# Inverse roots of the differential tiles by VectorE instead of a reciprocal and a ScalarE square root

## The chip, the core and the metric

The kernel runs on one core of a Trainium2 chip. The core has five engines with queues of their own: TensorE (PE, matmuls), VectorE (DVE), ScalarE (ACT, activation functions), GpSimd (POOL) and SyncE (SP, issues DMAs). They meet only at semaphores. The metric is the device time of one execution in microseconds; lower is better.

## The reference, cut to what matters

Two transformer blocks follow each other on a sequence of 512 tokens of width 1024, all in float32. The second block has three attention branches; one is differential attention with 4 heads of value width 64:

```python
def diff_branch(dq, dk, dv, pos, qn_g, kn_g, lam_vecs, subln_g, lam_init):
    ...
    def block_fn(qblk, start):
        sc = jnp.einsum('bqhmd,bkhmd->bhmqk', qblk, k).astype(jnp.float32) * scale
        sc = jnp.where(causal_mask(start, s)[None, None, None], sc, NEG_INF)
        p = jax.nn.softmax(sc, axis=-1)
        a = (p[:, :, 0] - lam * p[:, :, 1]).astype(v.dtype)
        return jnp.einsum('bhqk,bkhd->bqhd', a, v)

    o = causal_block_sweep(block_fn, q)
    o = rms_norm(o, subln_g) * (1.0 - lam_init)
    return o.reshape(b, s, DIFF_W)
```

`rms_norm` divides each head's 64 values of a token by the root of their mean square plus 1e-6. It is the inverse root of this last norm that the change computes in another way. The branch's output then goes with those of latent attention (8 heads) and memory attention (4 heads) through a gate and the output projection.

## The kernel before, in words

The program is one instruction stream per engine, written out by hand; the order in each stream is the order in the code, and semaphores (`wait_ge`, `then_inc`) order the engines against each other. `link` puts a wait for VectorE's own step counter behind an instruction, so that the next one may read its result. Weights come as 128x1024 units through RAW, split by ScalarE (WHI) and GpSimd (WLO) into a high and a low half, so that a float32 product is made of three TensorE passes (lines 1838 to 1840).

The change lies in the last stage but one, `attention("late")`. Its list LATE has 20 maps: 8 of latent heads, 8 of differential heads (two for each head) and 4 of memory heads. A loop counter i runs over the maps, and each engine does in step i the work of several maps at different stages:

- TensorE: scores of map i+2 (lines 1977, 1982, or 1838 to 1840), the transposes of map i's probabilities (line 2010), value matmuls of map i-1 (lines 2038, 2043).
- VectorE: bias and row maximum of map i+1 (`biased`, line 1347), which also reads the scores out of their PSUM bank, so that TensorE may write the next ones; then `normed` of map i (lines 1362, 1387, 1389); then what concerns finished maps (1265, 1462, 1464).
- ScalarE: copies of the transposed probabilities of map i-1 (line 875), exponentials of map i+1 (line 902), copies of finished outputs (945, 951).
- GpSimd: the widest scaling of a map (lines 685, 719, 725).

Two differential heads share a 128x512 tile, with the features in rows. There are two such tiles, and `diff_tile` names the step at which each is worked on. For a tile, ScalarE squares it (948); TensorE sums the squares over each head's 64 rows, turned so that tokens lie in partitions and SS gets 8 columns (2097, `dm_tot`); VectorE makes mean plus epsilon (1469) and the reciprocal (1470, `dm_rin`); ScalarE takes the root and spreads it by a broadcast of each column to 64 (862, into YSQ, `dm_rstd`); TensorE turns that back with an identity (2081, `dm_spread`); VectorE multiplies the tile by it and the gain (1413), then by the gate and a constant (1416, `dm_y`); ScalarE copies the high half (937, `dm_hi`), and VectorE makes the low one (1454, which the profile shows under the helper's line 1265). On ScalarE, line 862 stands at the head of its step, ahead of 875 and 902. On VectorE, lines 1469 and 1470 stand at the end of theirs, just ahead of the next map's bias adds. On TensorE, line 2081 stands behind the scores of map i+2.

ScalarE computes a function from a table that has to be loaded; the compiler puts an ACT_TABLE_LOAD ahead of an activation whose function isn't in the table loaded last.

Of the kernel before, what the change touches and what calls it, by code (L numbers as in the profile page):

```python
# [17 lines left out]
I32 = mybir.dt.int32  # L18
ALU = mybir.AluOpType
ACT = mybir.ActivationFunctionType  # L20
AX = mybir.AxisListType

P = 128
# [74 lines left out]
class Chain:  # L98
# [5 lines left out]
    def link(self, ins):  # L104
        self.n += 1
        ins.then_inc(self.sem, 1)
        self.eng.wait_ge(self.sem, self.n)


def build(nc, t, out):  # L110
    from contextlib import ExitStack
    ctx = ExitStack()
    with ctx:
# [41 lines left out]
        SS = sb("SS", [P, 64])  # L155
# [18 lines left out]
        YT, YSQ = PB[:, 5 * SEQ:6 * SEQ], PB[:, 6 * SEQ:7 * SEQ]  # L174
# [26 lines left out]
        def row(name, n):  # L201
# [46 lines left out]
        dm_sq, dm_tot, dm_rin, dm_rstd, dm_spread, dm_read, dm_y, dm_hi, dm_lo, k_mm = [sem(s) for s in  # L248
            ("dm_sq", "dm_tot", "dm_rin", "dm_rstd", "dm_spread", "dm_read", "dm_y", "dm_hi", "dm_lo", "k_mm")]
# [78 lines left out]
        for h in range(4):  # L328
            for m in range(2):
# [4 lines left out]
                               y=h, rows=slice(64 * (h % 2), 64 * (h % 2) + 64), ytile=Y_DM + h // 2, ztile=4 + h // 2,  # L334
# [9 lines left out]
        for h in range(NH):  # L344
# [4 lines left out]
                            y=h, rows=slice(64 * (h % 2), 64 * (h % 2) + 64), ytile=LQ + h // 2, ztile=h // 2,  # L349
# [5 lines left out]
        for maps in (ab, LATE):  # L355
            n = ng = nt = 0
# [374 lines left out]
        def _(act):  # L731
# [44 lines left out]
            for kt in range(KT):  # L776
                if kt == 2:
# [3 lines left out]
                    for b in range(5):  # L781
                        a, e = OH * b // 5, OH * (b + 1) // 5
                        ins = act.activation(FX[0:16, :, :].rearrange("p a b -> p (a b)")[:, a:e], PS[0:16, 2 + b, 0:e - a], ACT.Copy)
# [16 lines left out]
            for c in range(13):  # L800
                if c != 1:
                    stream(u + (c + 3 if c else 4))
                if c < 11:
# [5 lines left out]
                    else:  # L809
                        for g in range(2 if c == 8 else 1):  # L810
                            for half in (slice(0, 64), slice(64, 128)):
                                ins = act.activation(hi(K_AT[c][g])[half, :], ps[64 * g:64 * g + 64, :], ACT.Copy)
                        if c > 8:
                            ins = act.activation(key_raw(c), ps[64:128, :], ACT.Copy)
# [24 lines left out]
            for tk in range(NT):  # L839
                ins = act.activation(GATE[:, tk, :], PS[:, 4 + tk, 384:408], ACT.Sigmoid, scale=RT[:, tk:tk + 1])  # L840
# [14 lines left out]
            def attention(name):  # L855
                maps, pts = GROUP[name]
                A = ATT[name]
                for i in range(-1, len(maps) + (3 if name == "late" else 2)):
                    tile = diff_tile(maps, i - 4)
                    if tile is not None:  # L860
                        act.wait_ge(dm_rin, tile + 1)
                        act.activation(YSQ.rearrange("p (g e) -> p g e", g=8), SS[:, 0:8, None].broadcast_to([P, 8, 64]),
                                       ACT.Sqrt).then_inc(dm_rstd, 1)
                    if 0 <= i - 1 < len(maps) and maps[i - 1].get("mode") != "hold":
                        m = maps[i - 1]
                        if m["n"] > 2:
# [4 lines left out]
                        for g, qs in enumerate(m["groups"]):  # L871
                            act.wait_ge(A["turned"], m["t0"] + g + 1)
                            for q in [q for q in qs if q <= 4]:
                                for to, src in turned_aps(m, pt, q):
                                    ins = act.activation(to, src, ACT.Copy)  # L875
# [4 lines left out]
                    if name == "ab" and i == 2:  # L880
                        act.wait_ge(cmp_mm, 1)
                        for g in range(2):
                            kc = slice(KC + 32 * g, KC + 32 * g + 32)
                            for half in (slice(0, 64), slice(64, 128)):
                                ins = act.activation(hi(22)[half, kc], PS[64 * g:64 * g + 64, 2, 32 * g:32 * g + 32], ACT.Copy)
                        ins.then_inc(cmp_hi, 1)
                    if name == "ab" and i == LATE_K:
                        act.wait_ge(A["scores"], ab[8]["g0"])
                        for ktile in (9, 10):
                            for half in (slice(0, 64), slice(64, 128)):  # L890
                                ins = act.activation(hi(K_AT[ktile][1])[half, :], key_raw(ktile), ACT.Copy)
                            ins.then_inc(late_hi, 1)
                    if i + 1 < len(maps):
                        m = maps[i + 1]
                        for g, qs in enumerate(m["groups"]):
                            act.wait_ge(A["biased"], m["g0"] + g + 1)
                            if 4 in qs:
                                ins = act.activation(prob_cmp(m), prob_cmp(m), ACT.Exp, scale=m["scale"])
                            for q in [q for q in qs if q < 4]:
                                nk = m["spans"][q][1]  # L900
                                dst = prob_of(m, q)
                                ins = act.activation(dst, dst, ACT.Exp, bias=stat(m, NMAX)[:, q:q + 1], scale=-1.0,  # L902
                                                     accum_out=stat(m, SUM)[:, q:q + 1])
                        if m.get("sink"):
                            ins = act.activation(stat(m, SINK), stat(m, NMAX), ACT.Exp,
                                                 bias=row("sinks", 8)[:, m["h"]:m["h"] + 1])
# [14 lines left out]
                    if name == "ab" and 0 <= i - 2 < len(maps) and maps[i - 2]["last"]:  # L921
# [3 lines left out]
                        for half, qs in halves(m):  # L925
                            ins = act.activation(blocks_of(yt[rows, :], qs), blocks_of(PS[half:half + DH, m["bank"], :], qs), ACT.Copy)
# [274 lines left out]
        def _(dve):  # L1201
            chain = Chain(dve, dve_step)
            link = chain.link
# [37 lines left out]
            for kt in range(KT):  # L1241
                dve.wait_ge(n_hi, kt + 1)
                dve.scalar_tensor_tensor(out=HLO[:, kt, :], in0=X[:, kt, :], scalar=col("g_mix", kt),  # L1243
                                         in1=HHI[:, kt, :].bitcast(F), op0=ALU.mult, op1=ALU.subtract).then_inc(n_lo, 1)
# [22 lines left out]
            for c in range(11):  # L1267
# [9 lines left out]
                else:  # L1277
                    for g in range(2 if c == 8 else 1):
                        rows = slice(64 * g, 64 * g + 64)
                        for half in (slice(0, 64), slice(64, 128)):  # L1280
                            ins = low_from_psum(lo(K_AT[c][g])[half, :], hi(K_AT[c][g])[rows, :], ps[rows, :])
# [69 lines left out]
            def normed(A, m):  # L1351
# [24 lines left out]
                for qs in m["groups"][:2] if "latent" in m else m["groups"][:1] if "pair" in m else m["groups"]:  # L1376
# [12 lines left out]
                            ins = dve.tensor_scalar(ap, ap, w, None, ALU.mult)  # L1389
                    ins.then_inc(A["normed"], 1)  # L1390

            def attention(name):
                maps, pts = GROUP[name]
                A = ATT[name]
                for i in range(-1, len(maps) + 3):
# [5 lines left out]
                    if name == "ab" and i == 2:  # L1401
# [5 lines left out]
                        for q in range(NT):  # L1407
                            ins = dve.tensor_copy(v_cmp(q)[32 * q:32 * q + 32, :], PS[0:32, 2, P:2 * P])
                        ins.then_inc(cmp_lo, 1)
                    tile = diff_tile(maps, i - 4)  # L1410
                    if tile is not None:
                        dve.wait_ge(dm_spread, tile + 1)
                        dve.scalar_tensor_tensor(out=YT, in0=YT, scalar=col("subln"), in1=PS[:, DIFF_BANK[tile], :],
                                                 op0=ALU.mult, op1=ALU.mult).then_inc(dm_read, 1)
                        dve.wait_ge(dm_read, tile + 1)
                        dve.scalar_tensor_tensor(out=YT, in0=YT, scalar=1.0 - LAM_INIT, in1=FX[:, 4 + tile, :],
                                                 op0=ALU.mult, op1=ALU.mult).then_inc(dm_y, 1)
# [5 lines left out]
                    if name == "ab" and 0 <= i - 3 < len(maps) and maps[i - 3]["last"]:  # L1423
# [3 lines left out]
                        for half, qs in halves(m):  # L1427
                            ins = low_from_psum(blocks_of(yl[rows, :], qs), blocks_of(yh[rows, :], qs),
                                                blocks_of(PS[half:half + DH, m["bank"], :], qs))
# [13 lines left out]
                    if name == "ab" and i - 1 in UA_FILL:  # L1443
                        n = UA_FILL[i - 1]
# [21 lines left out]
                    if diff_tile(maps, i - 3) is not None:  # L1466
                        tile = diff_tile(maps, i - 3)
                        dve.wait_ge(dm_tot, tile + 1)
                        link(dve.tensor_scalar(SS[:, 0:8], PS[:, DIFF_BANK[tile], 0:8], 1.0 / 64, EPS, ALU.mult, ALU.add))
                        dve.reciprocal(SS[:, 0:8], SS[:, 0:8]).then_inc(dm_rin, 1)  # L1470

            attention("ab")


# [21 lines left out]
            for j in range(4):  # L1496
# [20 lines left out]
                for e in range(2):  # L1517
                    dve.wait_ge(merge_act, 4 * j + 3 + e)
                    n = 14 + 2 * j + e
# [909 lines left out]
```

## Time and profile before

| | |
|---|---|
| median of 3 runs | 1075.66 us (1074.31 to 1080.67) |
| profiled execution, its own time | 1074.28 us |
| its span | 1072.4 us |
| TensorE busy | 1025.3 us, 96% |
| VectorE busy | 606.8 us, 57% |
| ScalarE busy | 544.7 us, 51% |
| GpSimd busy | 407.8 us, 38% |
| mean granted TensorE clock | 0.987 |

The span is the time from the first to the last instruction in the profile of one execution; the execution's own time has 1.9 us around it. Busy shares are averages over stages with different limits. Line numbers are those of the kernel before.

### The profile page before, as it was taken

The numbers are of one execution on the slowest core, as the hardware profiler recorded it, in microseconds if no ns is written. First come the engines' busy times: TensorE is split into PE (matmuls) and PEld (weight loads), VectorE is DVE, ScalarE is ACT, GpSimd is POOL, SyncE is SP. The second block draws the span as 40 slices with busy tenths as digits, with TensorE's granted clock in tenths as the row PEclk, the third lists the DMA queues.
The fourth block names the chain that finished last, engine by engine and source line by source line (L and its number), as shares of the span: only waits on it lengthen the run. The fifth ranks groups of instructions, "written<-read, shape, count | busy, mean of one in ns | idle before, by whom it ended". The sixth has DMA issues, their size and how long they took to land.

```text
span 1072.4 us, 15098 instructions
## 1 busy us (share of the span) xinstructions
PE 1025.3 (96%) x5166; PEld 837.8 (78%) x5166; DVE 606.8 (57%) x1327; ACT 544.7 (51%) x1104; POOL 407.8 (38%) x211
## 2 busy tenths in 40 slices
PE   6999999999999999999999999999999889888798
PEld 4879788888778788888888888788887778666577
DVE  4547457988364665554545454433334988586732
ACT  5443666887433345444444444443334463977921
POOL 2456412001243444444444444415443334533332
PEclk9999999999999999999999999999999999899999
DMA  7564222111134322222222224233443134332213
GB/s 259 194 169 153 84 79 74 51 41 40 41 119 132 110 93 96 99 98 98 98 98 98 91 101 141 99 138 98 153 132 99 59 109 127 94 89 74 73 56 118
DMA packets 38812, 111.88 MB, mean 104 GB/s; under 512 B 5235, under 2 KB 8563, under 8 KB 38067
## 3 DMA queue, kind: packets, MB, share of 16 engines
q1 hardware_dynamic: 28572, 87.60, 25.1%
q10 hardware_dynamic: 8584, 18.89, 5.5%
q0 software_dynamic: 1600, 4.66, 1.2%
q8 instruction: 33, 0.54, 0.2%
q14 instruction: 23, 0.19, 0.1%
HBM read 100.25 MB, written 7.96 MB: 101 GB/s over the span
## 4 chain that ended last, share of the span: by engine, by line
issue 49%; PE 21%; POOL 14%; DVE 8%; ACT 5%; DMA 3%; POOLq 0%; ACTq 0%; DVEq 0%
POOL WLO L668 13%; PE PS L1838 6%; PE PS L1840 6%; PE PS L1839 6%; DMA RAW<-wstream 2%; ACT PB L902 1%; PE PS L2038 1%; ACT WHI L741 1%; PE PS L2188 1%; DMA X<-xT 1%; ACT HF L875 1%; PE PS L2010 1%; DVE PB L1387 1%; DVE PB L1347 1%; DVE FX L1647 1%
## 5 line engine op out<-in xcount | busy, mean ns | idle before, releaser
L668 POOL TENSOR_TENSOR WLO<-RAW,WHI 128x1024 fp32r<-128x1024 f32 x147 | 355.2, 2417 | 585.2 <-ACT WHI L741 585.0
L741 ACT ACTIVATE WHI<-RAW 128x1024 fp32r<-128x1024 f32 x154 | 162.8, 1058 | 282.1 <-PE PS L1840 261.6
L1838 PE MATMUL PS<-HHI,WHI 128*128 128x512 f32 x648 | 256.9, 396 | 9.9 <-DVE HLO L1243 8.6
L1840 PE MATMUL PS<-HHI,WLO 128*128 128x512 f32 x648 | 254.2, 392 | 0.0
L1839 PE MATMUL PS<-HLO,WHI 128*128 128x512 f32 x648 | 254.0, 392 | 0.0
L1838 PEld LDWEIGHTS PS<-HHI,WHI 128*128 128x128 f32 x648 | 123.0, 190 | 38.9 <-issue 12.1
L1838 PE MATMUL PS<-BHI,WHI 128*128 128x512 f32 x368 | 145.3, 395 | 3.5 <-POOL WLO L668 2.0
L1840 PE MATMUL PS<-BHI,WLO 128*128 128x512 f32 x368 | 143.4, 390 | 0.0
L1839 PE MATMUL PS<-BLO,WHI 128*128 128x512 f32 x368 | 143.3, 389 | 0.0
L1840 PEld LDWEIGHTS PS<-HHI,WLO 128*128 128x128 f32 x648 | 122.6, 189 | 26.1
L1839 PEld LDWEIGHTS PS<-HLO,WHI 128*128 128x128 f32 x648 | 123.0, 190 | 25.2 <-issue 0.5
L1225 DVE TENSOR_TENSOR PS<-PS,PB 128x512 f32<-128x512 f32 x63 | 43.9, 696 | 85.4 <-PE PS L1840 83.8
L1838 PEld LDWEIGHTS PS<-BHI,WHI 128*128 128x128 f32 x368 | 69.1, 188 | 21.1 <-issue 2.5
L1840 PEld LDWEIGHTS PS<-BHI,WLO 128*128 128x128 f32 x368 | 69.1, 188 | 14.7
L1839 PEld LDWEIGHTS PS<-BLO,WHI 128*128 128x128 f32 x368 | 69.2, 188 | 13.8
L902 ACT ACTIVATE PB<-PB,ST 128x256 f32<-128x256 f32 (+3 forms) x132 | 69.6, 544 | 0.6 <-DVE ST L1347 0.5
L1561 DVE SCALAR_TENSOR_TENSOR FX<-PS,CL,FX 128x511 f32<-128x511 f32 (+1 forms) x88 | 61.6, 742 | 13.4 <-ACT FX L1001 13.2
L2010 PE MATMUL PS<-IDN,PB 128*128 128x128 f32 x270 | 40.4, 291 | 11.3 <-DVE PB L1389 6.5
L1838 PE MATMUL PS<-WHI,HHI 128*128 128x512 f32 (+2 forms) x128 | 48.0, 375 | 2.7 <-ACT PB L1027 2.0
L1840 PE MATMUL PS<-WHI,HLO 128*128 128x512 f32 (+2 forms) x128 | 47.4, 370 | 0.0
L1839 PE MATMUL PS<-WLO,HHI 128*128 128x512 f32 (+2 forms) x128 | 47.3, 369 | 0.0
L2010 PEld LDWEIGHTS PS<-IDN,PB 128*128 128x128 f32 x270 | 32.7, 148 | 18.5 <-DVE PB L1389 5.3
(332 smaller groups left out, 1504.1 us busy)
## 6 DMA issues: line engine op xcount, KB each, us to landing
RAW<-wstream SPq DMA_DIRECT2D x154, 512.0 KB, 3.2
X<-xT ACTq DMA_DIRECT2D x4, 512.0 KB, 9.2
BF<-wstream POOLq DMA_DIRECT2D x2, 1024.0 KB, 6.7
BG<-wstream POOLq DMA_DIRECT2D x2, 1024.0 KB, 7.1
bias_b<-bias_rows ACTq DMA_DIRECT2D x2, 1024.0 KB
FX<-bias_b ACTq DMA_DIRECT2D x8, 256.0 KB, 2.6
X<-xT ACTq DMA_DIRECT2D x8, 256.0 KB, 3.6
x_keep<-X ACTq DMA_DIRECT2D x2, 1024.0 KB, 6.5
```

Of the source, the lines that this page charges most:

```text
L668: pool.tensor_tensor(WLO[:, s, :], RAW[:, s, :], WHI[:, s, :].bitcast(F), ALU.subtract).then_inc(split_lo, 1)
L741: act.activation(WHI[:, c % 2, :], RAW[:, c % 2, :], ACT.Copy).then_inc(split_hi, 1)
L875: ins = act.activation(to, src, ACT.Copy)
L902: ins = act.activation(dst, dst, ACT.Exp, bias=stat(m, NMAX)[:, q:q + 1], scale=-1.0, accum_out=stat(m, SUM)[:, q:q + 1])
L1225: dve.tensor_tensor(PS[:, bank, :], PS[:, bank, :], RSTD, ALU.mult).then_inc(scaled, 1)
L1347: ins = dve.tensor_tensor_reduce(prob_of(m, q), PS[:, b, o:o + nk], bias_of(m, q), -m["scale"], init, ALU.add, ALU.min, stat(m, NMAX)[:, q ...
L1387: ins = dve.scalar_tensor_tensor(out=ap, in0=ap, scalar=w, in1=o, op0=ALU.mult, op1=ALU.add)
L1561: dve.scalar_tensor_tensor(out=y, in0=PS[:, 2 * e + s, 0:SEQ - sh], scalar=cv[:, tap:tap + 1], in1=y, op0=ALU.mult, op1=ALU.add).then_inc( ...
L1838: pe.matmul(dst, a[0], b[0], start=first, stop=False, **kw)
L1839: pe.matmul(dst, a[0], b[1], start=False, stop=False, **kw)
L1840: return pe.matmul(dst, a[1], b[0], start=False, stop=last, **kw)
L2010: ins = pe.transpose(PS[:, 3 + b, o + j * P:o + (j + 1) * P], pr[:, p0:p0 + P], IDN[:, :])
```

## The change

The root moves to VectorE. A new helper `inverse_root` takes a first value of the inverse root from the number's bits read as an integer (-0.5 times the bits plus a constant), and improves it in three Newton steps of three operations each. VectorE thus issues ten operations on 128x8 where it issued one reciprocal, and each but the last is linked. The result is in columns 8 to 15 of SS, and columns 16 to 23 are scratch. ScalarE's line 862 becomes a Copy with the same broadcast, of 128x512.

```diff
@@ -859,8 +859,8 @@
                         act.wait_ge(dm_rin, tile + 1)
-                        act.activation(YSQ.rearrange("p (g e) -> p g e", g=8), SS[:, 0:8, None].broadcast_to([P, 8, 64]),
-                                       ACT.Sqrt).then_inc(dm_rstd, 1)
+                        act.activation(YSQ.rearrange("p (g e) -> p g e", g=8), SS[:, 8:16, None].broadcast_to([P, 8, 64]),
+                                       ACT.Copy).then_inc(dm_rstd, 1)
@@ -1389,6 +1389,17 @@
+            def inverse_root(x, y, t):
+
+                link(dve.tensor_scalar(y.bitcast(I32), x.bitcast(I32), -0.5, float(0x5F3759DF), ALU.mult, ALU.add))
+                for n in range(3):
+                    link(dve.tensor_tensor(t, y, y, ALU.mult))
+                    link(dve.scalar_tensor_tensor(out=t, in0=t, scalar=-0.5, in1=x, op0=ALU.mult, op1=ALU.mult))
+                    ins = dve.scalar_tensor_tensor(out=y, in0=t, scalar=1.5, in1=y, op0=ALU.add, op1=ALU.mult)
+                    if n < 2:
+                        link(ins)
+                return ins
+
@@ -1467,7 +1478,8 @@
                         link(dve.tensor_scalar(SS[:, 0:8], PS[:, DIFF_BANK[tile], 0:8], 1.0 / 64, EPS, ALU.mult, ALU.add))
-                        dve.reciprocal(SS[:, 0:8], SS[:, 0:8]).then_inc(dm_rin, 1)
+                        root = inverse_root(SS[:, 0:8], SS[:, 8:16], SS[:, 16:24])
+                        root.then_inc(dm_rin, 1)
```

ScalarE's instructions around the first differential tile, before (YSQ is a part of PB; HF takes the turned probabilities):

```order
L951 ACTIVATE BHI<-PS 64x512
L862 ACT_TABLE_LOAD
L862 ACTIVATE PB<-SS 128x512
L875 ACTIVATE HF<-PS 128x2x128
L875 ACTIVATE HF<-PS 128x128
L875 ACTIVATE HF<-PS 128x3x128 x2
L875 ACTIVATE HF<-PS 128x128
L902 ACT_TABLE_LOAD
L902 ACTIVATE PB,ST<-PB,ST 128x256
```

and of the change at the same place:

```order
L951 ACTIVATE BHI<-PS 64x512
L862 ACTIVATE PB<-SS 128x512
L875 ACTIVATE HF<-PS 128x2x128
L875 ACTIVATE HF<-PS 128x128
L875 ACTIVATE HF<-PS 128x3x128 x2
L875 ACTIVATE HF<-PS 128x128
L902 ACTIVATE PB,ST<-PB,ST 128x256
```

Both table loads are gone; the second tile loses its two in the same way, and all else is in the same order.

VectorE at the first tile, before (L1347 is the bias add and maximum of the next map):

```order
L1464 TENSOR_TENSOR PS<-PS,FX 64x256
L1469 TENSOR_SCALAR SS<-PS 128x8
L1470 RECIPROCAL SS<-SS 128x8
L1347 ISA PB,ST<-PS,TRI 128x256
L1347 ISA ST 128x1
```

and of the change, where lines behind the new helper have numbers higher by 11:

```order
L1480 TENSOR_SCALAR SS<-PS 128x8
L1394 TENSOR_SCALAR SS<-SS 128x8
L1396 TENSOR_TENSOR SS<-SS 128x8
L1397 SCALAR_TENSOR_TENSOR SS<-SS 128x8
L1398 SCALAR_TENSOR_TENSOR SS<-SS 128x8
L1396 TENSOR_TENSOR SS<-SS 128x8
L1397 SCALAR_TENSOR_TENSOR SS<-SS 128x8
L1398 SCALAR_TENSOR_TENSOR SS<-SS 128x8
L1396 TENSOR_TENSOR SS<-SS 128x8
L1397 SCALAR_TENSOR_TENSOR SS<-SS 128x8
L1398 SCALAR_TENSOR_TENSOR SS<-SS 128x8
L1347 ISA PB,ST<-PS,TRI 128x256
```

The ten operations stand where the reciprocal stood, ahead of the bias adds in VectorE's queue.

## Rows read from the trace of the kernel before

**Rows 1.** ScalarE's instruction groups: line, operation, count, busy us, mean ns, idle before.

```profile
L862 ACT ACT_TABLE_LOAD x2 | 2.6, 1283 | 0.0
```

**Rows 2.** The chain of waits, 974 to 1013 us: start, length, what it went through.

```profile
975.15 0.39 ACT L862
975.54 0.90 issue
...
978.46 1.28 ACT L902
...
983.20 0.42 DVE PB L1347
...
985.11 4.28 POOL PB L719 x4
...
1004.76 1.11 ACT L862
...
1007.79 1.28 ACT L902
...
1012.44 0.43 DVE PS L1462
```

**Rows 3.** Timeline of tile 1: start, length, instruction, idle before and its releaser.

```profile
975.08 0.17 DVE L1469 TENSOR_SCALAR SS<-PS 128x8 f32<-128x8 f32 x1 [0.63 <-PE PS L2097]
...
975.28 0.20 DVE L1470 RECIPROCAL SS<-SS 128x8 f32<-128x8 f32 x1
975.43 0.42 DVE L1347 CUSTOM_DVE_ANT_0 PB<-PS,TRI 128x256 f32<-128x256 f32 x1
...
977.08 0.08 DVE L1347 DVE_READ_ACCUMULATOR2_ANT ST<- 128x1 f32 x1
...
977.22 0.29 PEld L1982 LDWEIGHTS PS<-BLO,BHI 128*128 128x128 f32 x1 [0.32 <-DVE ST L1347]
...
977.38 2.04 PEld L2081 LDWEIGHTS PS<-IDN,PB 128*128 128x128 f32 x8
...
979.76 0.75 DVE L1413 SCALAR_TENSOR_TENSOR PB<-PB,CL,PS 128x512 f32<-128x512 f32 x1 [1.59 <-PE PS L2081]
...
980.54 0.69 DVE L1416 SCALAR_TENSOR_TENSOR PB<-PB,FX 128x512 f32<-128x512 f32 x1
...
981.95 0.61 ACT L937 ACTIVATE BHI<-PB 128x512 fp32r<-128x512 f32 x1
...
982.59 0.69 DVE L1265 TENSOR_TENSOR BLO<-PB,BHI 128x512 fp32r<-128x512 f32 x1 [0.77 <-ACT BHI L937]
```

**Rows 4.** Timeline of tile 2.

```profile
1005.61 0.20 DVE L1470 RECIPROCAL SS<-SS 128x8 f32<-128x8 f32 x1
...
1007.11 0.08 DVE L1347 DVE_READ_ACCUMULATOR2_ANT ST<- 128x1 f32 x1
...
1007.46 0.19 PEld L1838 LDWEIGHTS PS<-BHI 96*128 96x128 f32 x1
...
1008.10 1.09 PEld L2081 LDWEIGHTS PS<-IDN,PB 128*128 128x128 f32 x8
...
1009.42 0.75 DVE L1413 SCALAR_TENSOR_TENSOR PB<-PB,CL,PS 128x512 f32<-128x512 f32 x1 [1.49 <-PE PS L2081]
...
1010.81 0.68 DVE L1265 TENSOR_TENSOR BLO<-PS,BHI 64x512 fp32r<-64x512 f32 x1
...
1011.63 1.08 PE L2038 MATMUL PS<-HF,BF 128*64 128x256 f32 x8 [1.07 <-DVE BLO L1265]
```

**Rows 5.** Timeline of VectorE in the rope angles, a linked chain of small operations.

```profile
296.98 0.23 DVE L1488 SCALAR_TENSOR_TENSOR COS<-KR,COS 128x64 f32<-128x64 f32 x1
297.24 0.49 DVE L1490 SCALAR_TENSOR_TENSOR COS<-KR,COS 128x64 f32<-128x64 f32 x2
```

**Rows 6.** Busy us in two stretches, then granted clock (PEclk), DMA share, GB/s.

```profile
978.00:980.00 2.00, 2.00 (x12) 2.00 (x11) 0.41 (x2) 1.97 (x4) 1.51 (x1) 0.50 0.16 66
...
1008.00:1010.00 2.00, 1.92 (x16) 1.59 (x15) 0.58 (x1) 1.99 (x5) 1.82 (x2) 1.00 0.00 0
```

## The prediction

> **What bounds the kernel now.** I read the page first. Over the whole span TensorE is the busiest engine, but the edited lines run in one short stage, the late attention (about 924 to 1025 us), so that stage decides, not the span's shares. Next came the instruction groups of ScalarE. Line 862, the edited one, carries two table loads of 1.28 us [rows 1]; with a square root gone from between exponentials, its return load goes too. Then the chain of waits through the two places where line 862 runs. There the chain is mostly ScalarE's: at the first place the load of line 862 and the wait for it take 0.39 + 0.90 us, and the exponentials behind it pay 1.28 us for getting their table back; at the second 1.11 and 1.28 us [rows 2]. So four loads lie on the chain as it stands, and a reader may be tempted to book them as gain. The timeline of the two places shows what runs just beside that chain [rows 3, 4]. I call the places tile 1 (975 to 983 us) and tile 2 (1005 to 1012 us).
>
> In tile 1 VectorE makes mean plus epsilon at 975.08 and the reciprocal at 975.28, and from 975.43 the bias adds of the next map (line 1347). Their last accumulator read ends at 977.16. TensorE's last score matmul waits for just that (0.32 us idle, released by ST of line 1347), and its next work, at 977.38, is line 2081, which spreads the roots. VectorE's line 1413 waits 1.59 us for line 2081, then comes 1416, then ScalarE's 937, then VectorE's copy of the low half, then the next bias adds at 983.20, which stand on the chain [rows 2, 3]. A second path, VectorE to TensorE to VectorE, thus runs beside ScalarE's with little slack. This is the path that the edit lengthens.
>
> **The change, part by part.** *Table loads removed.* Copy runs between exponentials without a load already (line 875 does, all through the stage), and the instruction order has no load left there: four fewer, 4 x 1.28 = 5.1 us of ScalarE busy time. The load of line 862 was partly hidden, though: it began at 975.15, and the reciprocal that ScalarE waited for anyway ended only at 975.48 [rows 2, 3].
>
> After each load the next activation starts within 0.02 us: 978.46 + 1.28 gives 979.74, and the exponentials start at 979.75 in the chain. The Trainium skill (ScalarE: Activation LUTs, "What ACT_TABLE_LOAD costs") says 1283 ns for the load and some 1380 ns of drain besides, 2.66 us for a switch. The load agrees with the row; by the drain, ScalarE's path would win 1.38 us more in each tile than I book. The trace shows no such gap here, so by that rule my sum would be wrong on ScalarE's path alone.
>
> *Ten VectorE instructions for one.* The reciprocal (0.20 us) is replaced by ten operations on 128x8, nine of them followed by a wait for VectorE's own semaphore. A step of this kind takes 0.20 us from start to start: 975.08 to 975.28, duration 0.17 [rows 3]. The bounds are 0.17 (its duration, no gap) and 0.26 (a linked scalar-tensor-tensor of 128x64, 296.98 to 297.24 [rows 5]); I take 0.20, since width and engine fit. The tenth operation has nothing chained to it, like the reciprocal now, and takes its place (0.15 to the next start). So VectorE reaches the bias adds 9 x 0.20 = 1.80 us later, and ScalarE's release comes at 975.28 + 1.80 + 0.17 = 977.25 and 1007.58 instead of 975.48 and 1005.81.
>
> *ScalarE's path.* Line 862 starts 0.08 us after the release: 977.33 against 976.44 now, +0.89; the return load is gone, -1.30; the exponentials start 0.41 us earlier. In tile 2: 1007.66 against 1006.05, +1.61 - 1.30 = 0.31 us later [rows 2, 4]. On this path alone the change is worth -0.1 us: it swaps its waits.
>
> *VectorE's queue.* Behind the chain stand the bias adds, which free score banks for TensorE. In TensorE's order the scores come ahead of line 2081, so the spread waits for them though its input is ready. **Tile 1:** bias end 977.16 to 978.96, line 2081 to 979.18, line 1413 from 979.76 to 981.56, line 1416's end from 981.23 to 983.03. ScalarE's 937 now starts at 981.95, held by ScalarE's own work, 0.72 us after its input; it will start at 983.11, +1.16. The low half and the bias adds at 983.20 move with it [rows 3]. From there the chain goes through VectorE to GpSimd's four scalings (4.28 us) and on, without room that I can see, so **+1.16** is carried to tile 2 [rows 2]. **Tile 2:** bias end 1007.19 to 1008.99; the score matmuls that need it start now at 1007.46 (0.27 us after, TensorE was busy until then), and would at 1009.04: +1.58. With it go line 2081 (1008.10), 1413 (1009.42), the low half at 1010.81, the value matmuls at 1011.63 that waited 1.07 us for it, and line 1462 at 1012.44, on the chain [rows 2, 4]: **+1.58**. Behind it VectorE is the bound up to the output projection, which is dense TensorE work and carries the shift to the end.
>
> Sum: 1.16 + 1.58 = **+2.7 us**. Nothing else moves: TensorE, GpSimd and the DMA queues issue what they did, and the scratch columns 8 to 23 of SS are used by nobody then.
>
> Against the profiled execution (1074.28 us) that is 1077.0. The median of the three runs is 1.4 us above that execution, which would give 1078.4. I say 1077.5, between the two.
>
> **Rivals.**
> *A, ScalarE's path decides* (-0.1 to +1.7). Where the shifted TensorE work finishes sooner than I move it, ScalarE sets the time. There is something for it: in tile 1 the granted clock around line 2081 was 0.50, in tile 2 it was 1.00 [rows 6], and its load-weights span was 2.04 us against 1.09 [rows 3, 4]. 0.50 is the 1.2 GHz level, 1.00 is 2.4; TensorE had waited for bias adds just before. If 1.80 us later the clock is back, 0.95 us of tile 1's shift is returned: 0.2 + 1.6 = +1.8, 1076.1. If tile 2 also finds cover, 1074.2. Against: in tile 2 the line was at full clock already and has no second to return.
> *B, slower still: the clock falls in tile 2.* The edit makes TensorE wait 1.6 us more before line 2081 there. If the clock then drops as it did in tile 1, line 2081 takes 0.95 us longer on the path: +3.7, and with steps of 0.26 instead of 0.20 (0.54 more in each tile) +4.7: 1078.0 to 1079.0, or 1080.4 from the median. It decides where the granted clock between 1006 and 1012 falls to 0.50; it is the case on the slower side, should my forecast count as no change.
> *C, faster: the loads on the chain are simply gone.* 0.39 + 1.28 + 1.11 + 1.28 = 4.06 us [rows 2] gives 1070.2. It needs the VectorE chain to be free and the path over 2081 to have 2 us of slack, from the point where line 862 starts before 976. The timeline speaks against both: VectorE ran nothing beside the chain that could be postponed, and line 937's slack is 0.72 us.
> *D, the loads stay*, the compiler putting one at the copy. The instruction order shows none; then ScalarE's own path is 0.89 and 1.61 us late beside the other (1.16 and 1.58), +2.8 us, 1077.1.
>
> **How the numbers follow.** My forecast 45%, A 28%, B 18%, C 5%, D 1%, the rest for what I do not see. About 1% (10.8 us) is what a measurement of this kernel can tell from no change: its three runs lie 6.4 us apart. All cases lie inside that, so no change takes nearly everything: 0.97, with 0.015 for each side. The range goes from A's best, 1074.2 less a few tenths for the runs' scatter, to B from the median: 1073.8 to 1080.4. It leaves out C and a run as high as the highest of the three.
>
> **What the profile after would show.** Right: two fewer table loads at line 862 and two fewer at 902; ten operations of 0.17 to 0.2 us, their starts 0.20 apart; line 862 at some 977.3, waiting idle on VectorE for about 2 us; the exponentials at 979.3; line 937 now idle on VectorE, and the bias adds of 983.20 at 984.3; line 1462 of tile 2 at 1015.2 (1012.44 + 2.7). Wrong: line 1413 starting within 1 us of today's time (then A), a clock of 0.50 in tile 2 (B), or steps over 0.26 us. The forecast as a whole fails if the span moves by more than 5 us in either direction, since no term here reaches that far.

## The result, and the profile after

| | before | the change |
|---|---|---|
| median of 8 runs | 1076.01 us (1074.31 to 1080.67) | 1080.24 us (1078.49 to 1082.71) |
| profiled execution, its own time | 1074.28 us | 1080.1 us |
| its span | 1072.4 us | 1078.3 us |
| VectorE busy | 606.8 us | 610.0 us |
| ScalarE busy | 544.7 us | 539.4 us |
| mean granted TensorE clock | 0.987 | 0.976 |

The ratio is 1.0046, with a 95% interval of 1.0034 to 1.0058. That is 4.9 us more (1076 x 0.0046), between 3.7 and 6.2. The change is slower, by less than 1%. The forecast had 1077.5, 1.8 us above the median it started from. It had the direction, and less than half of the size.

The edit itself came out as written. In ScalarE's groups of the kernel after, line 862 has no table load any more, and line 902 has two where the kernel before had four:

```profile
L902 ACT ACT_TABLE_LOAD x2 | 2.6, 1283 | 0.0
```

The timeline of tile 1 after (lines behind the helper are 11 or 12 higher; 1480 is the old 1469, 1994 the old 1982, 2093 the old 2081, 1424 the old 1413), to be read against [rows 3]:

```profile
974.55 0.17 DVE L1480 TENSOR_SCALAR SS<-PS 128x8 f32<-128x8 f32 x1 [0.63 <-PE PS L2109]
974.75 0.17 DVE L1394 TENSOR_SCALAR SS<-SS 128x8 int32<-128x8 int32 x1
...
974.96 0.17 DVE L1396 TENSOR_TENSOR SS<-SS 128x8 f32<-128x8 f32 x1
975.16 0.17 DVE L1397 SCALAR_TENSOR_TENSOR SS<-SS 128x8 f32<-128x8 f32 x1
...
976.56 0.17 DVE L1398 SCALAR_TENSOR_TENSOR SS<-SS 128x8 f32<-128x8 f32 x1
976.71 0.42 DVE L1347 CUSTOM_DVE_ANT_0 PB<-PS,TRI 128x256 f32<-128x256 f32 x1
976.76 0.63 ACT L862 ACTIVATE PB<-SS 128x512 f32<-128x512 f32 x1 [2.16 <-DVE SS L1398]
...
977.20 0.29 PEld L1994 LDWEIGHTS PS<-BLO,BHI 128*128 128x128 f32 x1 [2.77 <-DVE ST L1347]
...
978.66 2.04 PEld L2093 LDWEIGHTS PS<-IDN,PB 128*128 128x128 f32 x8
...
981.03 0.75 DVE L1424 SCALAR_TENSOR_TENSOR PB<-PB,CL,PS 128x512 f32<-128x512 f32 x1 [1.59 <-PE PS L2093]
...
982.54 0.63 ACT L937 ACTIVATE BHI<-PB 128x512 fp32r<-128x512 f32 x1 [1.62 <-DVE PB L1427]
...
983.81 0.42 DVE L1347 CUSTOM_DVE_ANT_0 PB<-PS,TRI 128x256 f32<-128x256 f32 x1
```

The ten operations take 0.17 us each and start 0.20 us apart, as forecast. ScalarE waits 2.16 us idle ahead of line 862. TensorE's weight loads, which waited 0.96 us before the first scores, now wait 2.77 us. The row of before for that:

```profile
975.91 0.19 PEld L1982 LDWEIGHTS PS<-BLO,BHI 128*128 128x128 f32 x1 [0.96 <-DVE ST L1347]
```

From the mean plus epsilon to the bias adds of the next step it was 983.20 - 975.08 = 8.12 us; it is 983.81 - 974.55 = 9.26 us. That is +1.14 where the prediction had +1.16.

The chain of waits after, in tile 1, no longer goes through ScalarE's table loads and exponentials [rows 2]. It goes through VectorE's queue and TensorE:

```profile
977.88 1.41 PE PS L1994 x3
979.29 1.72 PE PS L2093 x8
...
981.03 0.76 DVE PB L1424
...
981.82 0.70 DVE PB L1427
...
982.54 0.64 ACT BHI L937
```

Tile 2 after, by the timeline, against [rows 4]:

```profile
1007.48 0.17 DVE L1480 TENSOR_SCALAR SS<-PS 128x8 f32<-128x8 f32 x1 [1.94 <-PE PS L2109]
...
1010.44 0.29 PEld L1850 LDWEIGHTS PS<-BHI 96*128 96x128 f32 x1 [1.64 <-DVE ST L1347]
...
1011.90 0.33 PEld L1850 LDWEIGHTS PS<-BHI 96*128 96x128 f32 x1
...
1013.07 2.04 PEld L2093 LDWEIGHTS PS<-IDN,PB 128*128 128x128 f32 x8
...
1015.44 0.75 DVE L1424 SCALAR_TENSOR_TENSOR PB<-PB,CL,PS 128x512 f32<-128x512 f32 x1 [3.62 <-PE PS L2093]
```

Here much more was lost. From mean plus epsilon to line 1413's multiplication of the tile (now 1424) it was 1009.42 - 1005.41 = 4.01 us; it is 1015.44 - 1007.48 = 7.96 us, +3.95 where I forecast +1.58. A weight load of the scores takes 0.33 us instead of 0.19, and line 2093's loads take 2.04 us instead of 1.09. Busy times and granted clock in stretches of 2 us (busy us of TensorE, weight loads, VectorE, ScalarE, GpSimd; then the granted clock) show at what clock this work ran, and show a further low stretch that I had not expected, at 993:

```profile
992.00:994.00 2.00, 0.83 (x6) 0.53 (x5) 1.92 (x8) 0.92 (x3) 0.00 (x0) 0.75 0.00 0
994.00:996.00 2.00, 2.00 (x10) 2.00 (x11) 1.93 (x9) 2.00 (x10) 0.96 (x1) 0.50 0.41 70
...
1008.00:1010.00 2.00, 1.02 (x9) 0.42 (x4) 1.73 (x12) 0.31 (x1) 0.00 (x0) 1.00 0.00 0
1010.00:1012.00 2.00, 1.55 (x6) 1.56 (x7) 1.78 (x11) 2.00 (x8) 0.09 (x1) 0.51 0.00 0
1012.00:1014.00 2.00, 2.00 (x8) 1.71 (x7) 0.00 (x0) 1.36 (x6) 1.74 (x2) 0.50 0.00 0
1014.00:1016.00 2.00, 2.00 (x11) 2.00 (x11) 0.56 (x1) 0.00 (x0) 0.00 (x0) 0.50 0.00 0
```

Around line 2081 of tile 2 the clock was 1.00 before [rows 6]. After, TensorE is busy for 1.02 of the 2 us from 1008, and when it starts again at 1010.4 the clock is 0.50, 1.2 instead of 2.4 GHz, until about 1016.8. The work that runs at half the clock is the path: scores, then 2093, on which VectorE waits 3.62 us with everything behind it.

Three lengths per profile divide what follows tile 1, and I use them for all runs: from mean plus epsilon of tile 1 to that of tile 2, from there to the first matmul of the output projection, and from there to the end (47.0 to 47.1 us in every run). Each is the difference of two starts in that run's timeline. Each profile is one execution, so a single difference of a few tenths of a us says little.

| profile | tile 1 to tile 2 | tile 2 to projection |
|---|---|---|
| before | 30.33 | 19.93 |
| the change | 32.93 | 23.75 |

### The profile page after: what moved, and what is told of

It is laid out like the page before. It is cut to its first block, busy times and chain, and to the rows that moved or that the text cites. A ratio compares the mean times of both kernels' runs of the same rounds, so it can differ in the third digit from the quotient of the medians.

```text
span 1078.3 us, 15112 instructions
## 1 busy us (share of the span) xinstructions
PE 1030.6 (96%) x5166; PEld 843.6 (78%) x5166; DVE 610.0 (57%) x1345; ACT 539.4 (50%) x1100; POOL 408.0 (38%) x211
## 3 DMA queue, kind: packets, MB, share of 16 engines
HBM read 100.25 MB, written 7.96 MB: 100 GB/s over the span
## 4 chain that ended last, share of the span: by engine, by line
issue 48%; PE 25%; POOL 14%; DVE 8%; ACT 2%; DMA 2%; POOLq 0%; ACTq 0%; DVEq 0%
POOL WLO L668 13%; PE PS L1850 7%; PE PS L1852 6%; PE PS L1851 6%; PE PS L2022 1%; PE PS L2050 1%; PE PS L2200 1%; DMA RAW<-wstream 1%; DVE PB L1347 1%; DMA X<-xT 1%; PE PS L2055 1%; ACT WHI L741 1%; DVE PB L1387 1%; DVE FX L1659 1%; DVE FX L1655 0%
```

## The experiments

The theory after the result, called theory A in the texts below (it is not rival A of the prediction): the loads lie beside the path and are worth next to nothing; the ten operations delay VectorE's queue and through it TensorE (2.7 us); and TensorE's longer wait makes the granted clock fall in work on the path (the rest). The rivals: the loads do count, and something else costs yet more (their rival B); or the change has a fixed price whatever the length of the chain; or the clock has no part. All ratios are to runs of the kernel before on the same chip, and 0.001 is 1.08 us.

### Each half alone

`loads_only` leaves out the root: the reciprocal of before stays on VectorE, and only this changes:

```diff
-                                       ACT.Sqrt).then_inc(dm_rstd, 1)
+                                       ACT.Copy).then_inc(dm_rstd, 1)
```

> The reciprocal of before, spread by a Copy instead of a Sqrt: the roots are left out, so the four table loads are gone and nothing is added to VectorE. Theory A (VectorE's queue sets the path, the loads lie beside it): ScalarE comes 0.9 us earlier at tile 1's exponentials and line 937 can start at most 0.7 us earlier there and 0.1 us in tile 2, so -0.8 us against before (ratio 0.999). Rival B (the loads on the chain are worth what the chain says): -4 us (ratio 0.996).

Measured: 0.9995 (0.9981 to 1.0008), -0.5 us. Four table loads, 5.1 us of ScalarE, are worth 2 us at most (the interval's lower end), against the 4 us of the chain. In its tile 1 line 937, which ScalarE's own work held by 0.72 us before, waits 0.78 us for VectorE:

```profile
978.28 0.20 DVE L1470 RECIPROCAL SS<-SS 128x8 f32<-128x8 f32 x1
...
978.52 0.63 ACT L862 ACTIVATE PB<-SS 128x512 f32<-128x512 f32 x1 [0.39 <-DVE SS L1470]
...
980.32 1.29 PEld L2081 LDWEIGHTS PS<-IDN,PB 128*128 128x128 f32 x8
...
983.46 0.63 ACT L937 ACTIVATE BHI<-PB 128x512 fp32r<-128x512 f32 x1 [0.78 <-DVE PB L1416]
```

In this profile the next bias adds come 984.73 - 978.08 = 6.65 us after mean plus epsilon, where before it was 8.12. About half of that gain is not the table loads': the clock was still 1.00 when line 2081 began, its weight loads took 1.29 us instead of 2.04, and line 1413 started 3.87 us after mean plus epsilon instead of 4.68. The other half is the slack ahead of line 937, so removing the table loads does gain something here, but little; over the whole kernel it does not stand out from the noise.

`chain_only`: the change, but line 862 stays a Sqrt, of columns 8 to 15, so that what it spreads is not the inverse root:

```diff
-                                       ACT.Copy).then_inc(dm_rstd, 1)
+                                       ACT.Sqrt).then_inc(dm_rstd, 1)
```

> The ten VectorE operations of the change, but line 862 stays a Sqrt (so what it spreads isn't the inverse root), and the four table loads stay. Theory A: the loads are hidden beside VectorE's path, so this is as slow as the change, before +4.2 us (ratio 1.004), within 0.7 us of it. Rival B: the change as it is got 1 to 4 us back from the loads, so without that this is before +5 to +8 us (ratio 1.005 to 1.0075).

Measured: 1.0038 (1.0020 to 1.0056), +4.1 us. With its table loads back the kernel is as slow as the change (1.0046) and not slower, so no gain from the loads' removal shows beside the chain (the two intervals leave room for 1 to 2 us). In tile 2 the load runs at 1010.13 to 1011.41 and line 862 starts at 1013.13, idle before it, because VectorE's tenth operation ends only at 1013.10:

```profile
1010.13 1.28 ACT L862 ACT_TABLE_LOAD   x1
...
1012.93 0.17 DVE L1398 SCALAR_TENSOR_TENSOR SS<-SS 128x8 f32<-128x8 f32 x1
1013.13 0.63 ACT L862 ACTIVATE PB<-SS 128x512 f32<-128x512 f32 x1 [1.72 <-DVE SS L1398]
```

### Each tile alone

The change in one of the two tiles, the other as before (`tile == 0` for tile 1, `tile == 1` for tile 2; line 862 is a Copy of columns 8 to 15 in the changed tile and a Sqrt of columns 0 to 7 in the other, which the cut below leaves out):

```diff
-                        root = inverse_root(SS[:, 0:8], SS[:, 8:16], SS[:, 16:24])
+                        root = inverse_root(SS[:, 0:8], SS[:, 8:16], SS[:, 16:24]) if tile == 0 else dve.reciprocal(SS[:, 0:8], SS[:, 0:8])
```

> The change made in tile 1 alone; tile 2 keeps reciprocal and Sqrt. Theory A with a lowered clock: 1.2 us of shift through VectorE's queue, and some 1 to 1.5 us more where the longer idle time of TensorE makes the granted clock fall in the stage behind it: +1.2 to +2.5 us. Without the clock's part: +1.2 us. Rival B: 0 or below, since two loads go.

> The change made in tile 2 alone. Theory A with a lowered clock: 1.6 us of shift, and 1.5 to 2.4 us more because the clock falls while line 2081 of tile 2 runs (2.0 us instead of 1.1 for its weight loads): +2.5 to +4 us, and a granted clock of 0.50 there. Without the clock's part: +1.6 us and a clock of 1.00 there.

Measured: tile 1 alone 1.0018 (1.0003 to 1.0032), +1.9 us; tile 2 alone 1.0030 (1.0011 to 1.0048), +3.2 us. Together 5.1, and the change is 4.9. The profiles:

| profile | tile 1 to tile 2 | tile 2 to projection |
|---|---|---|
| before | 30.33 | 19.93 |
| tile1_only | 31.47 (+1.14) | 20.07 |
| tile2_only | 30.63 | 22.13 (+2.20) |

In the profiles, tile 1 costs what the queue alone should cost, and tile 2 costs 0.6 us more than its 1.58. The profile of tile2_only has the low clock in tile 2:

```profile
1010.00:1012.00 2.00, 2.00 (x13) 1.87 (x13) 1.14 (x7) 2.00 (x8) 0.73 (x1) 0.92 0.00 0
1012.00:1014.00 2.00, 2.00 (x12) 2.00 (x11) 0.79 (x2) 0.71 (x4) 1.09 (x2) 0.50 0.00 0
1014.00:1016.00 2.00, 1.46 (x10) 1.00 (x11) 1.90 (x3) 0.63 (x1) 0.00 (x0) 0.72 0.00 0
```

Here TensorE takes up the scores again at 1009.80, and the clock falls only at about 1011.7; in the change it had fallen before the scores went on. So only line 2081 (here 2094) is slow:

```profile
1009.80 0.19 PEld L1851 LDWEIGHTS PS<-BHI 96*128 96x128 f32 x1 [1.64 <-DVE ST L1348]
...
1011.22 1.62 PEld L2094 LDWEIGHTS PS<-IDN,PB 128*128 128x128 f32 x8
```

Line 2094 starts 4.38 us after mean plus epsilon, against 2.69 us for line 2081 before: +1.69, which is the queue's part, measured while the clock was 1.00. In chain_only it is 4.40, with the fall at about 1015.5 and loads of 1.90 us. In the change it is 5.59, because there the scores were slow too. The size of tile 2's loss thus depends on where the fall lands.

### The length of the chain

One Newton step, and six (the cut shows the first; the second has 6 and 5 in these places):

```diff
-                for n in range(3):
+                for n in range(1):
...
-                    if n < 2:
+                    if n < 0:
```

> The change with one Newton step instead of three (four operations for the reciprocal; the root is less exact). VectorE's bias adds come 3 x 0.20 = 0.6 us late. Theory A: line 937's slack of 0.7 us in tile 1 covers it, tile 2 gets 0.4 us: before +0.4 us, -0.5 to +1 with the load's gain on ScalarE. Rival (a fixed cost of the change, whatever its length): before +3 to +4 us.

> The change with six Newton steps (19 operations): bias adds 18 x 0.20 = 3.6 us late. Theory A: 1.8 us more in each tile than the change, +3.6 us, so before +7.8 us, up to +9.5 if the clock stays low for longer. Rival (another wait than VectorE's queue sets the path, such as ScalarE's loads): less than 2 us more than the change.

Measured: one step 1.0004 (0.9992 to 1.0016), +0.4 us; six steps 1.0073 (1.0056 to 1.0090), +7.9 us. Both as theory A had them. From 4 to 10 to 19 operations the time goes +0.4, +4.9, +7.9. A fixed price of the change is out. The price is not even per operation either. In tile 1 the first 0.6 us of delay are free, by the slack ahead of line 937: the next bias adds of one_step come 8.07 us after mean plus epsilon, 8.12 before. From 4 to 10 operations the queue grows by 2.4 us over both tiles, and the time by 4.5; from 10 to 19 it grows by 3.6 us, and the time by 3.0. The profiles show what was added between 4 and 10: in tile 2 the clock is 1.00 up to line 1413 with one step, and falls ahead of it with three and with six.

### Keeping TensorE busy in the wait

Two matmuls that nothing reads, in the change and (as a control) in the kernel before, ahead of the scores of the step in question. They wait until VectorE has read the bank (`SUMS_READ` holds its step count there; the trace has two records for each such matmul):

```diff
+            def keep_busy(tile, n):
+                pe.wait_ge(dve_step, SUMS_READ[tile])
+                for _ in range(n):
+                    pe.matmul(PS[:, DIFF_BANK[tile], 128:512], IDN[:, :], TRI[:, 128:512], start=True, stop=True,
+                              skip_group_check=True)
...
+                    if diff_tile(maps, i - 4) is not None:
+                        keep_busy(diff_tile(maps, i - 4), 2)
                     if 0 <= i + 2 < len(maps):
                         scores(A, maps[i + 2])
```

> The change, with two matmuls of 128x384 more for each tile, whose result nothing reads, in the place where TensorE waits for the bias adds behind the ten operations (some 0.8 us each by the 0.27 us of a 128x128 transpose, 1.6 of 2.7 us of waiting). Theory A with the clock: the granted clock stays at 1.00 while line 2081 of tile 2 runs and 1.5 to 2.5 us come back: before +2 to +3 us. Rival (the clock plays no part, all of the loss is VectorE's queue): no better than the change, before +4.2 us or 0.5 more.

> The same two matmuls for each tile in the kernel before. TensorE waits 1 us or less there, so they push the scores back by 0.5 to 1 us in each tile; in tile 1 they may keep the clock up (0.50 from 977 to 981 in the trace of before), worth 0.9 us. Theory A with the clock: before -0.5 to +1 us. It is the control for the padding: what it costs where there is little to fill.

Measured: the change padded 1.0018 (1.0006 to 1.0031), +1.9 us; before padded 1.0002 (0.9989 to 1.0016). More work on TensorE made the change faster by 3 us: its interval and that of the change (1.0034 to 1.0058) do not meet. It is a little more than the 1.5 to 2.5 us that were expected back. The profile of the padded change has the clock at 1.00 from 974 to 1021, and the loads of line 2093 (here 2103) are back at 1.09 us. The mean granted clock over the whole span says the same for all runs and not for one profile alone: 0.975 to 0.981 in the change and 0.976 to 0.983 in six_steps, 0.983 to 0.989 in the padded change. The fillers (2077), then the scores' wait, then 2103, by the timeline:

```profile
1012.16 0.94 PEld L2077 LDWEIGHTS PS<-TRI,IDN 128*128 128x128 f32 x4 [0.39 <-DVE SS L1398]
...
1014.21 0.19 PEld L1852 LDWEIGHTS PS<-BHI 96*128 96x128 f32 x1 [0.35 <-DVE ST L1348]
...
1015.65 1.09 PEld L2103 LDWEIGHTS PS<-IDN,PB 128*128 128x128 f32 x8
...
1016.97 0.75 DVE L1425 SCALAR_TENSOR_TENSOR PB<-PB,CL,PS 128x512 f32<-128x512 f32 x1 [1.38 <-PE PS L2103]
```

Mean plus epsilon of this tile starts at 1011.25, so line 1413 (here 1425) comes 5.72 us after it: +1.71 against before, near the 1.58 of the queue alone, where the unpadded change had +3.95.

The control came out even, but not because the fillers do nothing there. From mean plus epsilon to line 1413, in the four profiles:

| profile | tile 1 | tile 2 |
|---|---|---|
| before | 4.68 | 4.01 |
| before_padded | 3.56 | 5.31 |
| the change | 6.48 | 7.96 |
| after_padded | 5.38 | 5.72 |

In tile 1 of before the clock was low, and the fillers give 1.1 us back; in tile 2 it was not, and they stand in the way for 1.3 us. In the change they give back 1.1 us in tile 1 and 2.2 us in tile 2. And the clock still falls later on in both padded profiles, in the wait of the last two maps: it is 0.50 from about 1022 to 1028 in the padded change, and from about 1018 to 1028 in the padded before, where before had it from about 1015 to 1021.

### Filling two other waits

Three matmuls of 128x512 ahead of the first transposes of the stage, and three ahead of those of the last map but one. `waits_filled_before` is the kernel before with these alone; `waits_filled_after` is the change with these and with the two of `keep_busy` for each tile:

```diff
+            def fill_wait(bank, n):
+                for _ in range(n):
+                    pe.matmul(PS[:, bank, :], IDN[:, :], TRI[:, :], start=True, stop=True, skip_group_check=True)
...
+                    if name == "late" and i in (0, DIFF_AT[1] + 5):
+                        fill_wait(7 if i == 0 else 5, 3)
```

> The kernel before, with three matmuls of 128x512 (some 1.1 us each) in two other waits of the late attention: ahead of the first transposes (TensorE waits 4.1 us at 925 to 929 in the trace of before, and the clock is 0.50 from 930 to 936) and ahead of the transposes of the first of the last two maps (3.1 us at 1012.7 to 1015.8, clock 0.50 from 1015 to 1021). Theory A with the clock (an idle stretch is paid again in the work behind it): both low stretches go, before -2 to -4 us. Rival (the clock falls somewhere else instead, or those matmuls weren't on the path): within 0.7 us of before.

> The change with those fillings and the two of 128x384 for each tile as well. Theory A with the clock: 2.7 us (VectorE's queue) above the filled kernel before, so before -1 to +1 us. Rival: no better than after_padded, before +1.9 us.

Measured: before filled 0.9978 (0.9968 to 0.9988), -2.4 us, with a median of 1074.44; the change with all fillers 0.9999 (0.9987 to 1.0012), -0.1 us. The first is the fastest version here and beats both kernels. Two stretches of its profile, and the same two of before:

```profile
930.00:932.00 2.00, 1.22 (x8) 0.74 (x9) 2.00 (x11) 2.00 (x9) 1.74 (x1) 1.00 0.40 98
...
1018.00:1020.00 2.00, 2.00 (x19) 1.47 (x18) 1.62 (x4) 0.82 (x3) 1.42 (x1) 1.00 0.73 291
```

and before:

```profile
930.00:932.00 2.00, 1.83 (x8) 1.83 (x9) 1.73 (x8) 1.29 (x6) 1.14 (x2) 0.50 0.43 106
...
1018.00:1020.00 2.00, 2.00 (x10) 1.14 (x10) 1.07 (x3) 1.23 (x4) 1.73 (x1) 0.50 0.92 371
```

From 1018 to 1020 TensorE is busy throughout in both. The same eight value matmuls, of the filled kernel and of before, by the timelines:

```profile
1017.94 1.08 PE L2040 MATMUL PS<-HF,BF 128*64 128x256 f32 x8
```

```profile
1018.70 1.98 PE L2038 MATMUL PS<-HF,BF 128*64 128x256 f32 x8
```

From tile 2 to the projection the filled kernel takes 18.45 us against 19.93. Filled against filled, the change costs 1.0 - 0.9978/0.9999 = 0.2%, 2.3 us (some 0.6 to 4 by the two intervals). That is near the 2.7 us of the prediction's working for VectorE's queue. It is no clean measure of the queue, since the fillers are not the same: the filled before still has its clock at 0.50 in tile 1 (line 1413 comes 4.68 us after mean plus epsilon there, as before), the filled change does not.

### The chain elsewhere in VectorE's queue

Mean, epsilon and the ten operations go behind the bias adds, ahead of the scalings (the lines are taken out in their old place, which the cut leaves out):

```diff
                     for f, j in steps:
+                        if f is normed and diff_tile(maps, i - 4) is not None:
+                            tile = diff_tile(maps, i - 4)
+                            dve.wait_ge(dm_tot, tile + 1)
+                            link(dve.tensor_scalar(SS[:, 0:8], PS[:, DIFF_BANK[tile], 0:8], 1.0 / 64, EPS, ALU.mult, ALU.add))
+                            root = inverse_root(SS[:, 0:8], SS[:, 8:16], SS[:, 16:24])
+                            root.then_inc(dm_rin, 1)
                         if 0 <= j < len(maps):
                             f(A, maps[j])
```

> The change with mean, epsilon and the ten operations moved behind the next map's bias adds in VectorE's queue, ahead of its scalings. TensorE gets its scores' banks as early as before, but the roots come some 1.7 us later still (979.0 instead of 977.25 in tile 1), and ScalarE waits for them with the exponentials behind it. Theory A: the chain isn't free there, only moved to ScalarE's path and the scalings; before +3 to +5 us, like the change. Rival (the bias adds' delay is all that costs): before +0 to +1 us.

Measured: 1.0015 (1.0004 to 1.0026), +1.6 us. A miss: below what theory A was written to expect (3 to 5 us), and by its middle value above the rival (0 to 1 us), which the interval (0.4 to 2.8) still touches. The timeline of its tile 2:

```profile
1006.75 0.42 DVE L1481 TENSOR_TENSOR PS<-PS,FX 64x256 f32<-64x256 f32 x1
...
1007.09 0.42 DVE L1347 CUSTOM_DVE_ANT_0 PB<-PS,TRI 128x256 f32<-128x256 f32 x1
...
1009.11 0.17 DVE L1413 TENSOR_SCALAR SS<-PS 128x8 f32<-128x8 f32 x1 [0.56 <-PE PS L2109]
...
1012.01 0.97 PEld L2093 LDWEIGHTS PS<-IDN,PB 128*128 128x128 f32 x8 [0.25 <-ACT PB L862]
...
1013.21 0.75 DVE L1430 SCALAR_TENSOR_TENSOR PB<-PB,CL,PS 128x512 f32<-128x512 f32 x1 [1.18 <-PE PS L2093]
```

(Line 1413 is mean plus epsilon in this kernel, and 1430 the multiplication of the tile.) The bias adds now start at once behind line 1481, where VectorE used to stand idle 1.94 us for TensorE's sums (the idle time ahead of 1480 in tile 2 after). I had priced the move as a swap and overlooked that it fills this wait. TensorE gets its scores in time, waits only 0.25 us ahead of 2093, and the clock there is 1.00: the loads take 0.97 us. In tile 1 of the same profile the clock does fall, from about 981.3 to 988. So the place of the chain in the queue is worth 3.3 us (1.0046 to 1.0015; the intervals do not meet), with the same ten operations.

### All profiles side by side

The last column is the mean granted clock from mean plus epsilon of tile 2 to line 1413 of that tile.

| profile | tile 1 to tile 2 | tile 2 to projection | clock in tile 2 |
|---|---|---|---|
| before | 30.33 | 19.93 | 1.00 |
| loads_only | 29.10 | 20.37 | 1.00 |
| one_step | 30.25 | 20.30 | 1.00 |
| tile1_only | 31.47 | 20.07 | 1.00 |
| waits_filled_before | 30.76 | 18.45 | 1.00 |
| chain_behind_bias | 29.96 | 20.07 | 1.00 |
| before_padded | 30.31 | 21.64 | 1.00 |
| after_padded | 30.35 | 21.51 | 1.00 |
| waits_filled_after | 30.35 | 20.16 | 1.00 |
| tile2_only | 30.63 | 22.13 | 0.88 |
| chain_only | 31.58 | 22.42 | 0.84 |
| the change | 32.93 | 23.75 | 0.66 |
| six_steps | 33.27 | 25.78 | 0.65 |

The clock fell in tile 2 in exactly the four kernels that have ten or more operations ahead of its bias adds and no fillers there. That makes the longer wait the likely cause of the fall, and not the chance of one profile.

## Why the prediction was wrong, by its own steps

**Table loads removed: right.** Four fewer, hidden for the most part; alone they gave 0.5 us (2 at most), not the 4.06 us that stand on the chain (rival C). Behind a load of before the next activation starts within 0.02 us (978.46 + 1.28, then 979.75). The Trainium skill (ScalarE: Activation LUTs, "What ACT_TABLE_LOAD costs") has a drain of some 1380 ns there; this trace shows none, so it had nothing to give back here.

**Ten operations for one: right.** A pitch of 0.20 us, 0.17 us each, 1.8 us on VectorE's queue.

**ScalarE's path: right.** Line 862 of tile 1 starts 0.03 us behind the tenth operation, and the exponentials of tile 1 start 978.62 - 974.55 = 4.07 us after mean plus epsilon, against 979.75 - 975.08 = 4.67 before: 0.60 us earlier where I had 0.41. It gained nothing, since line 937 then waits 1.62 us for VectorE.

**VectorE's queue, tile 1: right in size,** +1.14 against +1.16, in the change, in chain_only and in tile1_only alike (9.26 us to the bias adds in all three), and each time with the clock at 0.50 around line 2081, as it was before. Rival A's hope that this clock would be back did not come true.

**VectorE's queue, tile 2: the step that failed.** I carried the durations of before with the shift, at the clock of 1.00 that [rows 6] shows for them. The shift itself was right: line 2081 began 1.69 us later in tile2_only and 1.71 in chain_only, where I had 1.58. But the shift is also a wait of TensorE, and the clock fell in it: the term of +1.58 measured +3.82 in the change's profile (19.93 to 23.75), +2.49 in chain_only's (22.42) and +2.20 in tile2_only's. This was rival B, to which I gave 18% and 0.95 us; its sign, a clock of 0.50 between 1006 and 1012, came. The direction was argued (TensorE waits more, and in tile 1 the clock was low after a wait), and it deserved to be the main case. In the change's profile it was also too small: not line 2081 alone, but the scores ahead of it and the transposes behind it ran at half the clock.

**"Without room that I can see, so +1.16 is carried": right as far as it went,** but the change's own profile is 1.44 us longer than that between the tiles (32.93 - 30.33 - 1.16), and has its clock at 0.50 from 993 to 999.5. That is no fixed part of the price, and it does not take the chain to get it: tile1_only (31.47) has no such fall and chain_only (31.58) a shorter one from 998, while loads_only, tile2_only and waits_filled_before have one within 993 to 999 with the reciprocal of before in tile 1. Why the clock falls there in some executions stays open.

**The sum.** 2.7 us was VectorE's queue. Of it only 1.8 us reached the forecast: a difference belongs on the median it will be compared with (1075.66 + 2.7 = 1078.4), and I put 1077.5, between that and a profiled execution that happened to be fast. So two things are missing from the forecast's +1.8: these 0.9 us, and the price of the clock, which the sum had at nothing because the clock of before was 1.00 there. The measured 4.9 us less the queue's 2.7 leave 2.2 for it (1.0 to 3.5 by the interval), and 3.0 us come back when TensorE is kept busy in the two waits, of which some 1.1 are clock in tile 1 that the kernel before pays as well. How the 2.2 us divide between tile 2 and the place at 993 isn't settled, since each profile is one execution, and the falls lie elsewhere in each. By its own sign the forecast failed as a whole: the span moved by 5.9 us (1072.4 to 1078.3), and it allowed 5.

**The range** (1073.8 to 1080.4) holds 1080.24 only because it reached to B from the median.

## What to carry to other kernels

A term of the form "so many us later on the queue" is the price only while the engines behind it keep their speed: where the one that waits is TensorE, price the work behind the wait at the lower clock as well (here 1.6 us of queue became 2.2 to 3.8 in the profiles). A load or wait that stands on the chain is worth the distance to the next path beside it, not its length; build the one-sided kernel (here the loads alone) before paying for its replacement with another engine's time. And look where in the queue a small chain can stand in idle time: the same ten operations cost 4.9 us ahead of the bias adds and 1.6 us behind them.

## What the runs showed of the hardware

- Linked VectorE operations on 128x8 cost 0.17 us each and 0.20 us from start to start, alike for tensor-scalar, tensor-tensor, scalar-tensor-tensor and for integers read as numbers.
- Matmuls without a use, put where TensorE waits, made a kernel faster: by 3 us in the change and by 2.4 us in the kernel before. In the latter the granted clock stayed at 1.00 through 928 to 938, where it had been 0.50 for 6 us. Where there was little to fill (before_padded, 1.0002) they gave nothing.
- With the clock at 0.50 the eight 128x128 weight loads of line 2081 take 2.04 us; at 1.00 they take 1.09 us, or 0.97 us.
- A wait of 1.64 us, behind a short burst of scores, was followed by a clock of 0.50 in the change, already when TensorE went on; in tile2_only and chain_only the same wait (1.64 and 1.65 us) was followed by it only 1.9 and 1.6 us after TensorE had gone on.
